# A 2-layer gated and dilated-attention block and a second attention block on one core: the opening loads x ahead of constants and side inputs, sums squares in pairs, and takes the lambda products later

## The chip, the cores and the metric

The kernel runs on one core of one Trainium2 chip. The metric is the device time of one execution in microseconds. Three timed runs of the kernel before gave 1493.45, 1486.89 and 1493.67 us, median 1493.45. The execution that was profiled took 1486.86 us.

## The reference, cut to what matters

The reference applies two blocks to 512 tokens of width 1024. The first is a gated MLP layer and a dilated-attention layer, the second holds a forgetting attention, a differential attention and a feed-forward part. Each layer starts by a root-mean-square norm of x and a modulation by vectors that a conditioning input `c` gives. Only the start of the first layer and one scalar of the second block are touched here:

```python
def gmlp_layer(x, c, ada_w, ada_b, norm_g, w_in, sgu_g, w_s, b_s, w_out):
    shift, scale, gate = ada_mod(c, ada_w, ada_b, 3)      # silu(c) @ w + b, split
    h = rms_norm(x, norm_g) * (1 + scale) + shift         # x * rsqrt(mean(x*x) + EPS) * g ...
    u, v, z = jnp.split(h @ w_in, 3, axis=-1)             # 1024 -> 3 * 2048
    v = rms_norm(jax.nn.gelu(v), sgu_g)
    ...
# second block, used only in its differential attention:
lv = diff_lam[l].astype(jnp.float32)
lam = jnp.exp(jnp.sum(lv[0] * lv[1])) - jnp.exp(jnp.sum(lv[2] * lv[3])) + lam_init
```

## The kernel before, in words

x is kept transposed in SBUF as 8 tiles of 128 model columns by 512 tokens (`x[:, kt, :]`, kt from 0 to 7), and stays there to the end. Weights come in 1 MB chunks (`w_raw`), which ScalarE rounds to `w_hi` and VectorE subtracts to `w_lo` (`to_hi` L486, `to_lo` L910), so that each product is three TensorE matmuls. The modulation vectors come from products of `ada` weight tiles with silu(c) on VectorE, summed along the row (`unit` L918, `up_unit` L1037). The order is written out by hand: each engine has its own instruction list, and waits on semaphores at constants. DMAs are issued in order by SP (queue q1) and by ScalarE (queue q10).

The opening is this. SP issues (L390 to L398) c, the vectors `vecs` (gains and modulation biases), x in two halves of 1 MB, the first `ada_up` tile of 1 MB, two `w_first` chunks of 1 MB, then seven more `ada_up`. ScalarE issues (L527 to L532) the constants (identity, the all-ones tile, masks and EPS, 590 KB), `lam_rows` (128 KB), `bf_col`, `wf_raw` (32 KB) and `csil[1]`, which is c of the second block spread over 128 rows (512 KB).

TensorE spreads c over 128 rows by two matmuls with a one-row operand (L1603), and ScalarE takes silu of both halves (L536). ScalarE then loads its exp and log table (L537) and squares the 8 tiles of x as their half lands (L540). VectorE takes six small gains of `vecs` (L1051 to L1056), waits for the three small inputs (L1057), makes the two lambda products (L1059), and adds squares 1 to 6 one by one onto square 0 (L1065). TensorE sums over the rows by two matmuls with the all-ones tile: one over the sum, one over square 7 (L1606, L1608); its result is signalled by `sum_done`. ScalarE takes Ln, Exp and Square of it (`rstd_start` L493), VectorE ends the reciprocal root by one Newton step (`rstd_end` L953). Then, for each kt, VectorE multiplies x by it (`x_n`, L1070) and makes the two modulation sums of the tile (`up_unit`), ScalarE makes `h_full` (L550) and rounds it to `h_hi` (L552). TensorE takes each `h_full` tile into eight 256-column matmuls against `w_first` in full fp32 (L1629), two records each in the profile. This is the first part of the v projection. VectorE makes the `h_lo` tiles behind the loop (L1076).

After that loop ScalarE issues `ws_t` and `b_sp` (L554, L555, 512 KB each) and goes on to the gelu of the first v tiles (L565). VectorE masks `ws_t` by the causal constant (L1087), which needs both loads. The second value derived from the lambda products, `neg_lam`, was made at L1078 and is read only in the second block.

The lines that the diff touches and their names: `consts` and `K_*` (L105), SP's list (L390), ScalarE's list (L527 to L556 and behind L597), VectorE's list (L1050 to L1078, L1087, L1101, L1128), TensorE's list (L1604).

## Time and profile before

| | us |
|---|---|
| three timed runs | 1486.89, 1493.45, 1493.67 |
| the profiled execution | 1486.86 |
| its span on the core | 1485.1 |
| TensorE busy | 1447.9 (97%) |
| VectorE busy | 953.3 (64%) |
| ScalarE busy | 624.3 (42%) |
| mean granted TensorE clock | 0.996 |

The span is what the profile shows on the engines; the rest of the profiled execution's time, 1.76 us, lies around it. Engines are PE (TensorE matmul), PEld (its weight load), DVE (VectorE), ACT (ScalarE), POOL (GpSimd) and SP. A name such as ACTq stands for the issue of a DMA on that engine. L1519 is the helper that issues every matmul and L908 the helper of VectorE's three-operand operations, so these are told apart by their tiles.

### The profile page before, as it was taken

The page shows a single profiled execution, that of the slowest core. Times are in us where ns is not written, and L with a number is a line of the kernel's source. Part 1 is how long each engine was busy: PE and PEld are TensorE (multiplying, and loading weights), DVE is VectorE, ACT ScalarE, POOL GpSimd, SP SyncE. Part 2 cuts the span into 40 slices and gives each one's busy share as a digit, 9 for nine tenths or more (in the row PEclk, how much of TensorE's full clock was granted, in tenths as well). Part 3 has the DMA queues.
Part 4 walks back from the last instruction along what each step waited for, and adds up shares of the span by engine and source line. Part 5 has one row for each costly group of instructions (what it writes and reads, how often), then busy time and mean ns, then how long its engine had stood idle before and what let it go on. Part 6 is the DMA issues. An engine that isn't in the chain of part 4 may idle for free.

```text
span 1485.1 us, 19595 instructions
## 1 busy us (share of the span) xinstructions
PE 1447.9 (97%) x7404; PEld 1183.0 (80%) x7404; DVE 953.3 (64%) x1392; ACT 624.3 (42%) x916; POOL 124.8 (8%) x58
## 2 busy tenths in 40 slices
PE   5999999999999999999999999999899999999999
PEld 3998888888788688888877787777488888888887
DVE  5975777777888466666666868779777344332333
ACT  4734223332466444444444456655555232211221
POOL 0000100001100322222212100000020000000000
PEclk9999999999999999999999999999999999999999
DMA  9785544467622111111111232012021322222222
GB/s 378 302 344 201 185 183 170 169 242 284 265 75 86 61 63 51 56 55 56 57 57 57 85 115 86 29 60 84 1 102 70 113 85 103 95 98 101 85 92 78
DMA packets 34269, 181.06 MB, mean 122 GB/s; under 512 B 3865, under 2 KB 4121, under 8 KB 19618
## 3 DMA queue, kind: packets, MB, share of 16 engines
q1 hardware_dynamic: 32114, 175.22, 32.0%
q10 hardware_dynamic: 2096, 5.04, 1.0%
q8 instruction: 38, 0.62, 0.2%
q14 instruction: 21, 0.17, 0.0%
HBM read 178.14 MB, written 2.11 MB: 121 GB/s over the span
## 4 chain that ended last, share of the span: by engine, by line
PE 87%; DVE 6%; DMA 4%; issue 1%; ACT 1%; SPq 0%; ACTq 0%; DVEq 0%
PE acc L1519 75%; PE ada L1519 4%; PE norm L1519 4%; DMA ada_out<-in_ada 3%; PE turn L1519 2%; PE turn L1754 1%; DVE w_lo L915 1%; PE turn L1873 1%; DVE hx L908 1%; DMA wf_raw<-in_forget 1%; DVE hk_lo L908 0%; DVE s L908 0%; DVE ada_out L908 0%; DVE h_lo L908 0%; DVE stat L1373 0%
## 5 line engine op out<-in xcount | busy, mean ns | idle before, releaser
L1519 PE MATMUL acc<-h_hi,w_hi 128*128 128x512 f32 x984 | 400.8, 407 | 0.0
L1519 PE MATMUL acc<-h_hi,w_lo 128*128 128x512 f32 x984 | 383.8, 390 | 0.0
L1519 PE MATMUL acc<-h_lo,w_hi 128*128 128x512 f32 x984 | 383.5, 390 | 0.0
L915 DVE TENSOR_TENSOR w_lo<-w_raw,w_hi 128x2048 fp32r<-128x2048 f32 (+1 forms) x89 | 205.9, 2314 | 69.0 <-ACT w_hi L491 68.8
L491 ACT ACTIVATE w_hi<-w_raw 128x2048 fp32r<-128x2048 f32 (+1 forms) x106 | 200.7, 1893 | 117.1 <-PE acc L1519 117.0
L1519 PEld LDWEIGHTS acc<-h_hi,w_hi 128*128 128x128 f32 x984 | 184.9, 188 | 46.1 <-issue 9.0
L1519 PEld LDWEIGHTS acc<-h_lo,w_hi 128*128 128x128 f32 x984 | 185.0, 188 | 44.6 <-issue 8.1
L1519 PEld LDWEIGHTS acc<-h_hi,w_lo 128*128 128x128 f32 x984 | 184.7, 188 | 39.1
L445 POOL TENSOR_TENSOR w_lo<-w_raw,w_hi 128x2048 fp32r<-128x2048 f32 x17 | 77.3, 4548 | 322.4 <-ACT w_hi L491 322.4
L1519 PE MATMUL acc<-w_hi,h_hi 128*128 128x256 f32 x320 | 92.6, 289 | 0.0
L1519 PE MATMUL acc<-w_lo,h_hi 128*128 128x256 f32 x320 | 90.5, 283 | 0.0
L1519 PE MATMUL acc<-w_hi,h_lo 128*128 128x256 f32 x320 | 90.4, 283 | 0.0
L908 DVE SCALAR_TENSOR_TENSOR x<-acc,mods,x 128x512 f32<-128x512 f32 (+1 forms) x40 | 33.1, 829 | 82.4 <-PE acc L1519 82.4
L1519 PE MATMUL acc<-gu_hi,w_hi 128*128 128x512 f32 x176 | 68.5, 389 | 0.0
L1519 PE MATMUL acc<-gu_lo,w_hi 128*128 128x512 f32 x176 | 68.5, 389 | 0.0
L1519 PE MATMUL acc<-gu_hi,w_lo 128*128 128x512 f32 x176 | 68.5, 389 | 0.0
L908 DVE SCALAR_TENSOR_TENSOR gu<-tanh_g,acc 128x512 f32<-128x512 f32 x21 | 14.4, 688 | 82.9 <-PE acc L1519 82.8
L908 DVE SCALAR_TENSOR_TENSOR y_half<-norm,y_half 128x512 f32<-128x512 f32 x54 | 37.1, 687 | 47.1 <-ACT y_half L501 47.1
L1519 PEld LDWEIGHTS acc<-w_hi,h_hi 128*128 128x128 f32 x320 | 61.3, 191 | 3.3 <-issue 3.3
L884 ACT ACTIVATE gu_hi<-gu 128x512 f32 (+1 forms) x22 | 13.9, 633 | 117.1 <-DVE gu L908 117.1
L1519 PEld LDWEIGHTS acc<-w_lo,h_hi 128*128 128x128 f32 x320 | 61.3, 192 | 0.5 <-issue 0.5
L497 ACT ACTIVATE y<-norm,consts 128x512 f32<-128x512 f32 x54 | 37.0, 685 | 58.1 <-PE norm L1519 58.0
(256 smaller groups left out, 2574.7 us busy)
## 6 DMA issues: line engine op xcount, KB each, us to landing
w_raw<-in_weights SPq DMA_DIRECT2D x102, 1024.0 KB, 4.7
ada_v<-in_ada SPq DMA_DIRECT2D x32, 512.0 KB, 5.9
ada_raw<-in_ada SPq DMA_DIRECT2D x32, 512.0 KB, 6.0
ada_out<-in_ada SPq DMA_DIRECT2D x32, 512.0 KB, 6.4
ada_up<-in_ada_first SPq DMA_DIRECT2D x8, 1024.0 KB, 20.2
w_raw<-in_weights SPq DMA_DIRECT2D x4, 768.0 KB, 4.2
x<-in_x SPq DMA_DIRECT2D x2, 1024.0 KB, 9.4
w_first<-in_weights SPq DMA_DIRECT2D x2, 1024.0 KB, 16.3
```

The source lines that it names most:

```text
L445: nc.gpsimd.tensor_tensor(w_lo[par][:, :], w_raw[par][:, :], w_hi[par][:, :].bitcast(F32), ALU.subtract).then_inc(lo_done, 1)
L491: nc.scalar.activation(w_hi[par][:, 0:used], w_raw[par][:, 0:used], ACT.Copy).then_inc(hi_done, 1)
L497: nc.scalar.activation(y0[:, :], total, ACT.Ln, scale=1.0 / count, bias=eps_col).then_inc(ln_done, 1)
L884: nc.scalar.activation(gu_hi[:, f, :], gu[par][:, :], ACT.Copy).then_inc(guhi_done, 1)
L908: return nc.vector.scalar_tensor_tensor(out, in0, scalar, in1, op0, op1, **more)
L915: nc.vector.tensor_tensor(w_lo[par][:, 0:used], w_raw[par][:, 0:used], f32(w_hi[par][:, 0:used]), ALU.subtract)\
L1519: return nc.tensor.matmul(out, lhsT, rhs, start=start, stop=stop)
L1754: turned = nc.tensor.transpose(bank, s_b[:, P * b:P * b + P], ident)
L1873: turned = nc.tensor.transpose(T0[:, P * b:P * b + P], s_2[n % 3][:, 0, P * b:P * b + P], ident)
```

## The change

The constants are laid out anew, with the all-ones tile and EPS in front. ScalarE's opening loads only these 132 columns (128 partitions x 528 bytes), with a semaphore of their own. The rest of the constants, `csil[1]`, `lam_rows`, `bf_col` and `wf_raw` are issued behind the h loop, around `ws_t`. SP issues both halves of x ahead of `vecs`. The squares are added in four pairs, each into its even tile, and TensorE sums the four pair tiles by four matmuls. The exp and log table is loaded behind the squares. The lambda products stand behind the masking of `ws_t`, their Exp and `neg_lam` behind the statistics of v.

```diff
--- before.py
+++ after.py
@@ -98,14 +98,15 @@
     d = i + TOK - P - x
     slopes = np.broadcast_to(-np.array(SLOPES_B, np.float32), (P, 24))
     last = np.broadcast_to(np.array([EPS, 0.0, 0.0, 0.0]), (P, 4))
-    tiles = [ident, ones, half, causal_t, np.where(d >= 0, d, FAR), np.where(i >= j, 0.0, -FAR), slopes, last]
+    tiles = [ones, last, ident, half, causal_t, np.where(d >= 0, d, FAR), np.where(i >= j, 0.0, -FAR), slopes]
     return [np.concatenate(part, axis=1).astype(np.float32) for part in (tiles, blocks)]
 
 
-K_ID, K_ONE, K_HALF, K_TRI, K_DIST, K_MASK = 0, P, 2 * P, 3 * P, 4 * P, 4 * P + TOK
+K_ONE, K_EPS, K_ID = 0, P, P + 4
+K_HALF, K_TRI, K_DIST = K_ID + P, K_ID + 2 * P, K_ID + 3 * P
+K_MASK = K_DIST + TOK
 K_SLOPE = K_MASK + P
-K_EPS = K_SLOPE + 24
-NCONST = K_EPS + 4
+NCONST = K_SLOPE + 24
 
 
 def program(nc, d):
@@ -250,7 +251,7 @@
     def sem(name):
         return nc.alloc_semaphore(name)
 
-    vecs_loaded, consts_loaded, ws_loaded = sem("vecs_loaded"), sem("consts_loaded"), sem("ws_loaded")
+    vecs_loaded, ones_loaded, consts_loaded, ws_loaded = sem("vecs_loaded"), sem("ones_loaded"), sem("consts_loaded"), sem("ws_loaded")
     x_loaded = [sem("x_loaded0"), sem("x_loaded1")]
     small_loaded, blocks_loaded, stored = sem("small_loaded"), sem("blocks_loaded"), sem("stored")
     w_loaded = [sem("w_loaded0"), sem("w_loaded1")]
@@ -388,9 +389,9 @@
                 sp.dma_start(ada_up[kt % UP][:, :, :].rearrange("p e k -> p (e k)"), d["ada_first"][kt]).then_inc(ada_up_loaded[kt % UP], 16)
 
             sp.dma_start(c_in[:, :], d["c"]).then_inc(c_loaded, 16)
-            sp.dma_start(vecs[:, :], d["vecs"]).then_inc(vecs_loaded, 16)
             for half in range(2):
                 sp.dma_start(x[:, 4 * half:4 * half + 4, :], d["x"][:, 4 * half:4 * half + 4, :]).then_inc(x_loaded[half], 16)
+            sp.dma_start(vecs[:, :], d["vecs"]).then_inc(vecs_loaded, 16)
             ada_up_load(0)
             for par in range(2):
                 sp.dma_start(w_first[par][:, :, :].rearrange("p k n -> p (k n)"), weights[par]).then_inc(w_first_loaded[par], 16)
@@ -524,23 +525,16 @@
                 nc.scalar.activation(sq[m % 2][:, :], x[:, m, :], ACT.Square).then_inc(sq_ready, 1)
 
 
-            act.dma_start(consts[:, :], d["tiles"]).then_inc(consts_loaded, 16)
-            act.dma_start(lam_rows[:, :], d["diff_lam_2"][0].rearrange("a b -> (a b)").partition_broadcast(P)).then_inc(small_loaded, 16)
-            act.dma_start(bf_col[:, :], d["b_f_2"].rearrange("a h -> h a")).then_inc(small_loaded, 16)
-            act.dma_start(wf_raw[:, :, :], d["forget"]).then_inc(small_loaded, 16)
-
-            act.dma_start(csil[1][:, :], d["c_2"][0].partition_broadcast(P)).then_inc(c2_loaded, 16)
+            act.dma_start(consts[:, 0:K_ID], d["tiles"][:, 0:K_ID]).then_inc(ones_loaded, 16)
 
             for n in range(2):
                 act.wait_ge(c_spread_in, n + 1)
                 nc.scalar.activation(csil[0][:, TOK * n:TOK * n + TOK], G[n][:, :], ACT.Silu).then_inc(csil_ready, 1)
-            act.preload_act_table_set("natural_log_exp_and_others")
             for kt in range(KT):
                 act.wait_ge(x_loaded[kt // 4], 16)
                 nc.scalar.activation(sq_first[kt][:, :], x[:, kt, :], ACT.Square).then_inc(sq_ready, 1)
+            act.preload_act_table_set("natural_log_exp_and_others")
             rstd_start(N_X0, NB[:, :], DM)
-            act.wait_ge(lam_part, 2)
-            nc.scalar.activation(lam_two[:, :], lam_two[:, :], ACT.Exp).then_inc(lam_exp, 1)
             for kt in range(KT):
                 if kt == KT - 1:
                     to_hi(1, 0)
@@ -551,7 +545,12 @@
                 act.wait_ge(hx_done, kt + 1)
                 nc.scalar.activation(h_hi[:, kt, :], h_full[:, kt, :], ACT.Copy).then_inc(hhi_done, 1)
 
+            act.dma_start(csil[1][:, :], d["c_2"][0].partition_broadcast(P)).then_inc(c2_loaded, 16)
+            act.dma_start(consts[:, K_ID:NCONST], d["tiles"][:, K_ID:NCONST]).then_inc(consts_loaded, 16)
             act.dma_start(ws_t[:, :, :], d["spatial"]).then_inc(ws_loaded, 16)
+            act.dma_start(lam_rows[:, :], d["diff_lam_2"][0].rearrange("a b -> (a b)").partition_broadcast(P)).then_inc(small_loaded, 16)
+            act.dma_start(bf_col[:, :], d["b_f_2"].rearrange("a h -> h a")).then_inc(small_loaded, 16)
+            act.dma_start(wf_raw[:, :, :], d["forget"]).then_inc(small_loaded, 16)
             act.dma_start(b_sp[:, :, :], d["a_b_spatial"][0].rearrange("g t -> (g t)").partition_broadcast(P)
                           .rearrange("p (g t) -> p g t", g=GROUPS)).then_inc(small_loaded, 16)
 
@@ -595,6 +594,8 @@
             nc.scalar.activation(v_stat[:, 2, :], v_stat[:, 1, :], ACT.Exp, scale=-0.5).then_inc(v_stat_act, 1)
             act.wait_ge(v_stat_act, 2)
             nc.scalar.activation(v_stat[:, 3, :], v_stat[:, 2, :], ACT.Square, scale=math.sqrt(0.5 / AW)).then_inc(v_stat_act, 1)
+            act.wait_ge(lam_part, 2)
+            nc.scalar.activation(lam_two[:, :], lam_two[:, :], ACT.Exp).then_inc(lam_exp, 1)
 
 
             def uz_pair(u):
@@ -1047,6 +1048,10 @@
                 stt(gscale[:, kt:kt + 1], mods[:, SCALE_A + 2 * kt:SCALE_A + 2 * kt + 1], 1.0, vecs[:, G_A + kt:G_A + kt + 1],
                     ALU.add, ALU.mult).then_inc(gsa_done, 1)
 
+            for i in range(KT // 2):
+                dve.wait_ge(sq_ready, 2 * i + 2)
+                nc.vector.tensor_tensor(sq_first[2 * i][:, :], sq_first[2 * i][:, :], sq_first[2 * i + 1][:, :], ALU.add)\
+                    .then_inc(sq_added, 1 + i // 2)
             dve.wait_ge(vecs_loaded, 16)
             nc.vector.tensor_scalar(gains[:, 0:1], vecs[:, G_QB:G_QB + 1], P ** -0.5, None, ALU.mult)
             nc.vector.tensor_scalar(gains[:, 1:2], vecs[:, G_FQ:G_FQ + 1], 0.125, None, ALU.mult)
@@ -1054,15 +1059,6 @@
             nc.vector.tensor_scalar(gains[:, 3:4], vecs[:, G_DQ:G_DQ + 1], 0.125, None, ALU.mult)
             nc.vector.tensor_copy(gains[:, 4:5], vecs[:, G_DK:G_DK + 1])
             nc.vector.tensor_scalar(gains[:, 5:6], vecs[:, G_DN:G_DN + 1], 1.0 - LAM_INIT, None, ALU.mult).then_inc(gains_ready, 1)
-            dve.wait_ge(small_loaded, 48)
-            for n in range(2):
-                stt(lam_prod[:, 64 * n:64 * n + 64], lam_rows[:, 128 * n:128 * n + 64], 1.0,
-                    lam_rows[:, 128 * n + 64:128 * n + 128], ALU.mult, ALU.mult, accum_out=lam_two[:, n:n + 1]).then_inc(lam_part, 1)
-            for m in range(1, KT - 1):
-                dve.wait_ge(sq_ready, m + 1)
-                if m > 1:
-                    dve.wait_ge(sq_added, m - 1)
-                nc.vector.tensor_tensor(sq_first[0][:, :], sq_first[0][:, :], sq_first[m][:, :], ALU.add).then_inc(sq_added, 1)
             dve.wait_ge(csil_ready, 2)
             up_unit(0)
             rstd_end(N_X0, NB[:, :], DM, x_rstd)
@@ -1074,8 +1070,6 @@
             for kt in range(KT):
                 dve.wait_ge(hhi_done, kt + 1)
                 nc.vector.tensor_tensor(h_lo[:, kt, :], h_full[:, kt, :], f32(h_hi[:, kt, :]), ALU.subtract).then_inc(hlo_done, 1)
-            dve.wait_ge(lam_exp, 1)
-            stt(neg_lam[:, :], lam_two[:, 1:2], -LAM_INIT, lam_two[:, 0:1], ALU.add, ALU.subtract).then_inc(lam_ready, 1)
 
 
             ada_v_units(0, 0)
@@ -1085,6 +1079,10 @@
             dve.wait_ge(consts_loaded, 16)
             tri = consts[:, K_TRI:K_TRI + P].unsqueeze(1).broadcast_to([P, GROUPS, P])
             nc.vector.tensor_tensor(ws_t[:, :, :], ws_t[:, :, :], tri, ALU.mult).then_inc(ws_ready, 1)
+            dve.wait_ge(small_loaded, 64)
+            for n in range(2):
+                stt(lam_prod[:, 64 * n:64 * n + 64], lam_rows[:, 128 * n:128 * n + 64], 1.0,
+                    lam_rows[:, 128 * n + 64:128 * n + 128], ALU.mult, ALU.mult, accum_out=lam_two[:, n:n + 1]).then_inc(lam_part, 1)
             ada_v_units(1, 0)
             to_lo(2, 0)
             ada_v_units(1, 1)
@@ -1099,6 +1097,8 @@
             stt(v_stat[:, 4, :], v_stat[:, 0, :], AW * EPS, v_stat[:, 3, :], ALU.add, ALU.mult).then_inc(v_stat_dve, 1)
             dve.wait_ge(v_stat_dve, 2)
             stt(v_stat[:, 5, :], v_stat[:, 4, :], 1.5, v_stat[:, 2, :], ALU.subtract, ALU.mult, reverse0=True).then_inc(v_stat_dve, 1)
+            dve.wait_ge(lam_exp, 1)
+            stt(neg_lam[:, :], lam_two[:, 1:2], -LAM_INIT, lam_two[:, 0:1], ALU.add, ALU.subtract).then_inc(lam_ready, 1)
 
 
             def uz_pair(u, cond):
@@ -1125,7 +1125,6 @@
                                             f32(y_hi[:, j, :]).rearrange("p (c t) -> p c t", c=TB),
                                             ALU.subtract).then_inc(ylo_done, 1)
 
-            dve.wait_ge(small_loaded, 64)
             half_uz = W_UZ // 2 + (C2_UNIT - FIRST_UZ_UNIT) // (2 * UNITS_UZ)
             uz_pair(W_UZ // 2, 0)
             with dve.Fori(W_UZ // 2 + 1, half_uz) as u:
@@ -1601,11 +1600,11 @@
             pe.wait_ge(c_loaded, 16)
             for n in range(2):
                 mm(G[n][:, :], one_row[:, :], c_in[:, TOK * n:TOK * n + TOK], True, True).then_inc(c_spread_in, 1)
-            pe.wait_ge(consts_loaded, 16)
-            pe.wait_ge(sq_added, KT - 2)
-            mm(NB[:, :], ones, sq_first[0][:, :], True, False)
-            pe.wait_ge(sq_ready, KT)
-            mm(NB[:, :], ones, sq_first[KT - 1][:, :], False, True).then_inc(sum_done, 1)
+            pe.wait_ge(ones_loaded, 16)
+            for i in range(KT // 2):
+                pe.wait_ge(sq_added, (1, 2, 4, 6)[i])
+                last = mm(NB[:, :], ones, sq_first[2 * i][:, :], i == 0, i == KT // 2 - 1)
+            last.then_inc(sum_done, 1)
 
 
             def v_pair(u):
```

## Rows read from the trace of the kernel before

**Rows 1.** The page: busy time by engine; granted clock by slice; the last chain's shares.

```profile
PE 1447.9 (97%) x7404; PEld 1183.0 (80%) x7404; DVE 953.3 (64%) x1392; ACT 624.3 (42%) x916; POOL 124.8 (8%) x58
...
PEclk9999999999999999999999999999999999999999
...
PE 87%; DVE 6%; DMA 4%; issue 1%; ACT 1%; SPq 0%; ACTq 0%; DVEq 0%
```

**Rows 2.** The chain in order of time, opening (start us, us, what).

```profile
2.29 9.19 DMA wf_raw<-in_forget
...
11.50 0.38 DVE lam_prod L908 x4
11.88 0.62 DVE sq_first L1065
...
15.78 0.70 DVE sq_first L1065
16.48 0.14 issue
16.62 3.58 PE norm L1519 x4
20.19 5.17 issue
25.36 1.19 PE acc L1519 x2
26.55 0.85 PE turn L1519 x2
...
31.40 0.43 PE acc L1519 x2
...
55.58 14.51 PE acc L1519 x121
```

**Rows 3.** Timeline of the opening (start us, us, instructions, idle before and releaser).

```profile
1.14 0.37 SPq L391 DMA_DIRECT2D vecs<-in_vecs  x1
...
1.57 0.89 SPq L393 DMA_DIRECT2D x<-in_x  x2
...
2.41 3.75 PE L1519 MATMUL acc<-c_in,one_row 1*128 1x512 f32 x4 [2.41 <-DMA c_in<-in_c]
...
5.18 0.14 DVE L1056 TENSOR_SCALAR gains<-vecs 128x1 f32<-128x1 f32 x1
6.19 0.60 ACT L536 ACTIVATE csil<-acc 128x512 f32<-128x512 f32 x1 [1.07 <-PE acc L1519]
6.80 1.28 ACT L537 ACT_TABLE_LOAD   x1
9.51 2.19 ACT L540 ACTIVATE sq_first<-x 128x512 f32<-128x512 f32 x4 [1.42 <-DMA x<-in_x]
...
12.97 2.19 ACT L540 ACTIVATE sq_first<-x 128x512 f32<-128x512 f32 x4 [1.27 <-DMA x<-in_x]
16.39 1.22 DVE L908 SCALAR_TENSOR_TENSOR ada_up<-ada_up,csil 128x1024 f32<-128x1024 f32 x1
...
18.99 0.16 DVE L908 SCALAR_TENSOR_TENSOR gscale<-mods,vecs 128x1 f32<-128x1 f32 x1
...
34.17 0.68 DVE L1070 TENSOR_TENSOR x_n<-x,x_rstd 128x512 f32<-128x512 f32 x1
...
37.45 0.68 DVE L1070 TENSOR_TENSOR x_n<-x,x_rstd 128x512 f32<-128x512 f32 x1
```

**Rows 4.** Stretches: us, busy PE, PEld, DVE, ACT, POOL, PEclk, DMA share, GB/s.

```profile
3.00:3.50 0.50, 0.50 (x2) 0.11 (x1) 0.00 (x0) 0.27 (x1) 0.00 (x0) 1.00 1.01 406
...
4.50:5.00 0.50, 0.50 (x1) 0.08 (x1) 0.14 (x3) 0.49 (x2) 0.00 (x0) 1.00 0.49 57
...
10.00:15.00 5.00, 0.00 (x0) 0.00 (x0) 3.08 (x9) 3.73 (x8) 0.00 (x0) 1.00 1.02 425
...
25.00:30.00 5.00, 4.64 (x11) 3.77 (x12) 4.93 (x11) 2.33 (x4) 0.00 (x0) 0.50 1.02 423
```

**Rows 5.** The DMAs: the page's issues; tile x; issues from 27 to 50 us.

```profile
w_raw<-in_weights SPq DMA_DIRECT2D x102, 1024.0 KB, 4.7
...
DMA to landing us min/median/max: 7.9/9.4/10.9
...
ada_up<-in_ada_first SPq DMA_DIRECT2D x1, 1024.0 KB, 11.5
```

**Rows 6.** DMA packets by queue from 3 to 3.5 us, then from 5 to 5.5 us.

```profile
q10 hardware_dynamic: 43, 0.20, 100.5%
...
q10 hardware_dynamic: 31, 0.03, 46.3%
q1 hardware_dynamic: 4, 0.03, 16.4%
```

**Rows 7.** Timeline behind the opening.

```profile
4.09 23.57 SPq L388 DMA_DIRECT2D ada_up<-in_ada_first  x7
...
48.68 0.45 ACTq L555 DMA_DIRECT2D b_sp<-in_a_b_spatial  x1
...
53.02 0.38 ACT L565 ACTIVATE v<-acc 128x256 f32<-128x256 f32 x1 [2.58 <-PE turn L1519]
...
55.77 0.28 PE L1519 MATMUL acc<-w_hi,h_hi 128*128 128x256 f32 x1
...
58.04 0.28 PE L1519 MATMUL acc<-w_lo,h_hi 128*128 128x256 f32 x1
...
70.06 1.23 DVE L908 SCALAR_TENSOR_TENSOR ada_v<-ada_v,csil 128x1024 f32<-128x1024 f32 x1 [1.14 <-DMA ada_v<-in_ada]
...
74.97 2.29 DVE L915 TENSOR_TENSOR w_lo<-w_raw,w_hi 128x2048 fp32r<-128x2048 f32 x1
```

**Rows 8.** Stretch of 54 to 56 us (columns as in rows 4).

```profile
54.00:56.00 2.00, 2.00 (x13) 1.82 (x12) 2.00 (x5) 1.97 (x10) 0.00 (x0) 1.00 0.00 0
```

## The prediction

> **What bounds the kernel now.** I read the page first. TensorE is busy 97% of the span, its granted clock is near full in every slice, and it holds 87% of the chain that ended last [rows 1]. So only what shortens TensorE's own work, or lets it start sooner, moves the end. All edits but two small ones lie ahead of 77 us, so I read the chain in order of time next [rows 2]. It starts at the landing of `wf_raw` at 11.48 us, a small load of the second block that VectorE waits for ahead of its adds. The lambda products and six adds follow up to 16.48, two matmuls over the squares take 3.58, then 5.17 us pass to the first h matmul at 25.36. From there TensorE issues without a gap past 55.58. The reader is to see that nothing from c, the constants or the modulation weights stands on this chain, only a load that the opening's arithmetic doesn't use. Whatever brings the first h matmul forward moves all that follows, so long as loads and VectorE keep up with it.
>
> **When x lands.** x's two halves are issued from 1.57 us and land 7.9 and 10.9 us after their issue [rows 3, 5]: 9.5 and 12.9 us, which fits the squares' starts at 9.51 and 12.97 [rows 3]. Queue q10 (ScalarE's) holds all DMA engines from 3 to 3.5 us, and x's queue q1 has four packets from 5 to 5.5 us [rows 6]; around 4.5 us the engines are half busy and move 57 GB/s [rows 4]. With only the 66 KB of ones ahead and `vecs` behind, x goes out one place earlier, at 1.14 [rows 3]. A 1 MB load in the steady part lands in 4.7 us [rows 5], and one more MB takes 2.5 us at 425 GB/s [rows 4]: I take 5.8 us for the first half and 8.3 for the second. The other end is that x's slowness is its own: 1.14 + 7.9 = 9.0 and 12.5 us.
>
> The Trainium skill bears on this. In "DMA: Bandwidth & Descriptors", section "Queues, rings and completion order", it says that each DMA engine goes round-robin between queues that have work. By that rule x was slowed only by the bytes that shared the engines with it, and its own descriptors weren't late. Rows 6 speak against an even sharing in this opening: from 3 to 3.5 us only q10 has packets, though x was issued at 1.57. By the rule x would gain only the bytes that leave its way, some 1.2 MB or 2.8 us at 425 GB/s, and land near 7.2 and 9.8 us, and the total gain below would be some 4.0 us in place of 4.9.
>
> **The squares and their sum.** ScalarE ends the second silu at 6.79 and now squares at once, since the table load (1.28 us) goes behind the squares [rows 3]. There it runs beside the pair sums on TensorE; without that cover it would cost its 1.28. Four squares take 2.19 us [rows 3], so eight run from 6.8 to about 11.1. An add is 0.70 [rows 2]. Pair 0 is ready at 6.8 + 1.1 + 0.7 = 8.6, pair 1 at 9.7, pair 2 at 10.8, pair 3 at 11.9. VectorE has four adds in place of six and waits for no small load.
>
> TensorE now makes four matmuls and not two. Two took 3.58 us, so 1.79 each; the same kind of work at 256 columns takes 0.85 at the slow rate and 0.43 at the other [rows 2], with the granted clock at 0.50, which is 1.2 GHz, from 25 to 30 us [rows 4] and full in nearly all of the page's slices [rows 1]. A 512-column one at 1.79 is thus at the 1.2 GHz level. Four of them from 8.65 end at 8.65 + 7.16 = 15.8, and TensorE is their bound, not VectorE. If the clock rises while they run, as it did after 4.6 us of unbroken h matmuls in rows 2 and 4, the last ends by 14.4 to 14.9. If all ran at 2.4 GHz the end would be pair 3 plus one matmul, 11.9 + 0.9 = 12.8. Against 20.20 in the trace the sum comes 4.4 (all slow), 5.8 (last one and a half fast) or 7.4 us (all fast) earlier. I take 4.9, near the slow end, because both short bursts on TensorE in the opening (3.75 and 3.58 us) ran slow throughout [rows 3, 2].
>
> **From the sum to the first h matmul** the chain is unchanged: Ln, Exp, Square, two Newton steps, x_n, h_full, 5.17 us [rows 2]. The first `up_unit` and the gains must be done by then. The gains wait for `vecs`, now behind x, near 8.6 us, and come behind the adds at 11.9, and take 0.4 us; `up_unit(0)` took 16.39 to 19.15 [rows 3], 2.8 us, so 12.3 to 15.1, while VectorE's next work is due at 15.3 + 2.1. Covered; without the cover up to 0.4. The first h matmul moves from 25.36 to about 20.5.
>
> **The h loop.** TensorE needs 8 x 0.43 = 3.45 us for a tile at full clock and VectorE makes one each 3.28 us (34.17 to 37.45) [rows 2, 3]. TensorE stays the bound, hence the shift is kept. In the first 4.6 us the clock is low [rows 4], which costs 2.3 us now and will again; a shorter or longer low stretch moves the result by up to 1 us either way. Supply: DMA runs full at about 425 GB/s [rows 4], and `ada_up` 7, issued at 27.3, landed 11.5 us later at 38.8 [rows 7, 5]. SP's order makes `ada_up` 1 the sixth MB behind x's first half: counting back six times 2.47 us from 38.8, it landed at 24.0, just ahead of its use at 24.9. In the change x's second half is in at 8.3, then `vecs` (0.2) and four MB: 18.4 us, for a use at 24.93 - 4.9 = 20.0. The loads gain as much as the work, since 1.2 MB left their way. If x lands late, so do these, and so does the work.
>
> **The moved loads.** Seven DMAs are issued behind the h loop in place of two. Five issues of the kind took 0.36 to 0.60 us each, 2.3 us together, against ScalarE's wait of 2.58 us ahead of the first gelu [rows 7]. That just fits; without cover they'd delay the gelu, which TensorE needs only at its next accumulators, so I count zero, at most 0.5. Their extra 1.2 MB (524 KB of the constants, then 128, 32 and 512 KB) take 2.9 us of DMA time, where the engines now stand still from 54 to 56 us [rows 8], with the new loads done by about 51. Zero.
>
> **Lambda.** The products (0.38 us [rows 2]) go behind the mask of `ws_t`, where VectorE waits 1.14 us for `ada_v` [rows 7]: hidden. Their Exp and `neg_lam` stand behind the statistics of v, one tiny operation each like the gains (0.14 us [rows 3]), on engines that TensorE is not waiting for: zero, at most 0.3.
>
> **Sum.** -4.9 us, bounds -2.1 (x not earlier) to -7.4. From the profiled execution, 1486.86 us (1485.1 in the span), that is 1482.0. The three runs shown lie at two values: one agrees with the profiled one, two are 6.6 us above, for no reason that a trace shows. The median is one of the upper ones, so I forecast 1493.45 - 4.9 = 1488.5, and count the lower value, 1482.0, as nearly as likely.
>
> **Rivals.**
> 1. *x lands no earlier* (the change doesn't do what it says). For: before 5 us q1 moves next to nothing [rows 6]. Against: 57 GB/s around 4.5 us, with small packets of q10, says that q10 was in the way [rows 4]. Squares from 9.0, the first pair at 10.9, four slow matmuls end at 18.0: -2.1 us, 1491.3. By an even sharing of the engines -4.0, 1489.5. Together 0.20.
> 2. *TensorE is warm during the pair sums*, so that the squares set the end: -7.4 us, 1486.0 (1479.5 at the lower value). For: the four matmuls are one unbroken stretch of up to 7 us after the c matmuls. Against: both bursts of the opening ran slow. 0.12.
> 3. *Slower: the masking of `ws_t` waits.* VectorE now waits there for the constants and four small loads, issued last. Behind it stand the `ada_v` units and `w_lo` of the fifth chunk, which ends at 77.26; TensorE gets to it at 55.58 + 2 x 96 x 0.12 = 78.6 [rows 2, 7], where 0.12 is the spacing of 20 matmuls from 55.77 to 58.04. Each us by which these loads are late beyond 1.1 (the wait that is there) plus 1.3 costs one. To turn the gain into a loss they must land 7.3 us after VectorE gets there at 62.8, which is 26 us after their issue near 44; x in the crowded opening took 10.9 [rows 5]. 1495 us at 8 us late, 0.05.
> 4. The forecast, -3.5 to -6.4 us: 0.63.
>
> **Chances.** Against 1493.45 a change under 0.5% (7.5 us) can't be told from none. The gain by itself is 0.33%, so it falls within 0.5% unless the new kernel's median lies at the lower value, as it did in one of three runs and in the profiled one; I give that 0.42, most of all cases. Slower by over 0.5% only by rival 3: 0.05. The rest, 0.53, is no change. The range: 1480.5 (the forecast at the lower value, part of rival 2) to 1492.5 (rival 1 and a delayed gelu). The forecast's own range at the upper value is 1487 to 1490.
>
> **What would show it.** Right: squares in one run from about 6.8 us, `x` landing 4.7 and 7.2 us after issue, four norm matmuls without a gap from about 8.7 to 15.3, first h matmul near 20.5, the w_hi matmuls starting near 50.7 in place of 55.58, no wait ahead of L1087's successor. Wrong: a second square group that starts after 10 us, norm matmuls at 0.9 us each, a wait of VectorE for `ada_up`, or a gap of TensorE between 60 and 90 us.

## The result: some 6.4 us faster in the median, and the profile after

| | runs | median us | lowest to highest |
|---|---|---|---|
| before | 17 | 1489.58 | 1486.27 to 1493.67 |
| changed | 17 | 1483.14 | 1480.09 to 1487.30 |

The ratio is 0.9955, 95% interval 0.9944 to 0.9966: 5.1 to 8.3 us faster. Each kernel's own runs spread over 7 us, as much as the gain; the last part of the experiments says why. The profiled execution of the changed kernel took 1483.83 us, with a span of 1482.0, 3.1 under the span before.

The chain of the changed kernel in order of time (start us, us, what) answers to [rows 2]:

```profile
0.75 1.40 DMA c_in<-in_c
2.28 3.76 PE acc L1518 x4
6.06 0.60 ACT csil L532
6.66 1.04 ACT sq_first L535 x2
7.73 0.70 DVE sq_first L1053
8.57 5.95 PE norm L1518 x8
14.52 5.17 issue
19.68 1.19 PE acc L1518 x2
20.88 0.85 PE turn L1518 x2
...
23.44 0.48 PE acc L1518 x2
23.91 0.43 PE ada L1518 x2
```

No load of the second block heads it now. It starts with c, which TensorE spreads and ScalarE puts through silu, then two squares and one add; from 8.57 us TensorE has norm matmuls without a gap. The step of 5.17 us is untouched.

The timeline of the changed kernel (columns as in rows 3):

```profile
1.15 0.84 SPq L393 DMA_DIRECT2D x<-in_x  x2
...
6.06 0.60 ACT L532 ACTIVATE csil<-acc 128x512 f32<-128x512 f32 x1 [1.11 <-PE acc L1518]
6.56 4.25 ACT L535 ACTIVATE sq_first<-x 128x512 f32<-128x512 f32 x8
...
10.83 1.28 ACT L536 ACT_TABLE_LOAD   x1
10.91 0.69 DVE L1053 TENSOR_TENSOR sq_first<-sq_first,sq_first 128x512 f32<-128x512 f32 x1 [0.34 <-ACT sq_first L535]
...
11.89 1.22 DVE L909 SCALAR_TENSOR_TENSOR ada_up<-ada_up,csil 128x1024 f32<-128x1024 f32 x1
...
46.24 1.28 ACT L564 ACT_TABLE_LOAD   x1 [2.97 <-issue]
47.53 0.38 ACT L564 ACTIVATE v<-acc 128x256 f32<-128x256 f32 x1
...
49.27 0.38 PE L1518 MATMUL acc<-w_hi,h_hi 128*128 128x256 f32 x1
...
63.36 0.22 DVE L909 SCALAR_TENSOR_TENSOR lam_prod<-lam_rows 128x64 f32<-128x64 f32 x1
```

The eight squares run as one group, with no wait for x in between, where the old ones had two waits [rows 3]. The table load stands behind them, beside TensorE. The first gelu starts the moment its table load ends, with no wait for TensorE ahead of it, where it had waited 2.58 us before [rows 7]. The lambda products have no wait ahead of them.

How long x took in the changed kernel (to compare with rows 5):

```profile
DMA to landing us min/median/max: 4.9/6.0/7.0
```

The two halves of x, issued at 1.15 and near 1.6 us, landed near 6.05 and 8.6 us. A stretch of the same trace (columns as in rows 4) shows the DMA engines full already at 3.5 us:

```profile
3.50:4.00 0.50, 0.50 (x1) 0.10 (x1) 0.00 (x0) 0.00 (x0) 0.00 (x0) 1.00 1.01 426
```

### The profile page after: what moved, and what is told of

It is laid out like the page before. It is cut to its first block, busy times and chain, and to the rows that moved or that the text cites. A ratio compares the mean times of both kernels' runs of the same rounds, so it can differ in the third digit from the quotient of the medians.

```text
span 1482.0 us, 19599 instructions
## 1 busy us (share of the span) xinstructions
PE 1452.7 (98%) x7408; PEld 1185.6 (80%) x7408; DVE 952.0 (64%) x1390; ACT 624.1 (42%) x916; POOL 124.9 (8%) x58
## 3 DMA queue, kind: packets, MB, share of 16 engines
q10 hardware_dynamic: 2240, 5.04, 1.1%
## 4 chain that ended last, share of the span: by engine, by line
PE 89%; DVE 5%; DMA 3%; issue 1%; ACT 1%; SPq 0%; DVEq 0%; ACTq 0%
PE acc L1518 76%; PE ada L1518 4%; PE norm L1518 4%; DMA ada_out<-in_ada 3%; PE turn L1518 2%; PE turn L1753 1%; DVE w_lo L916 1%; PE turn L1872 1%; DVE s L909 1%; DVE ada_out L909 0%; DVE stat L1372 0%; DVE hx L909 0%; DVE h_lo L909 0%; DVE s_b L909 0%; DVE z_t L1226 0%
## 5 line engine op out<-in xcount | busy, mean ns | idle before, releaser
L885 ACT ACTIVATE gu_hi<-gu 128x512 f32 (+1 forms) x22 | 13.9, 633 | 117.1 <-DVE gu L909 117.1
L1518 PEld LDWEIGHTS acc<-w_hi,h_lo 128*128 128x128 f32 x320 | 61.3, 192 | 0.0
```

What stands on the lines that cost most here:

```text
L885: nc.scalar.activation(gu_hi[:, f, :], gu[par][:, :], ACT.Copy).then_inc(guhi_done, 1)
L1518: return nc.tensor.matmul(out, lhsT, rhs, start=start, stop=stop)
```

## The experiments

In all of them "first h" is the first matmul over `h_full` (25.36 us before, 19.68 in the changed kernel) and "the seam" the first w_hi matmul, right behind the h loop (55.23 and 49.27).

### Taking the parts away

**The lambda products alone** (kernel before, with the products, their Exp and `neg_lam` moved as in the change):

```diff
-            dve.wait_ge(small_loaded, 48)
...
             for m in range(1, KT - 1):
```

> The kernel before with one edit: the lambda products, their Exp and neg_lam stand where the change puts them; the order of the loads, the six serial adds and the two matmuls over the squares are the old ones. Theory A (the wait for wf_raw only covers other waits: squares 4 to 7 come at 13.5 to 15.1 us because x's second half lands at 12.9): the serial adds then end at about 15.9 in place of 16.48, the sum of squares at 19.6 in place of 20.20, first h matmul 24.8 in place of 25.36, about -0.6 us. Rival B (the load that heads the chain of waits is the cost; the chain gives its landing 9.2 us): the adds go with the first squares, at least 2 us come back, first h matmul below 23.4.

```profile
12.43 2.19 ACT L540 ACTIVATE sq_first<-x 128x512 f32<-128x512 f32 x4 [0.82 <-DMA x<-in_x]
13.09 2.29 DVE L1061 TENSOR_TENSOR sq_first<-sq_first,sq_first 128x512 f32<-128x512 f32 x3 [0.20 <-ACT sq_first L540]
15.53 3.75 PE L1518 MATMUL norm<-sq_first,consts 128*128 128x512 f32 x4 [9.26 <-DVE sq_first L1061]
```

These are rows of its timeline. First h came at 24.45, 0.9 us earlier and not 2; median 1490.23, ratio 1.0000 (0.9987 to 1.0014). The adds wait for the squares, and the squares for x's second half. Of the 0.9 us, 0.5 is that x's second half came sooner in this execution (squares at 12.43, and 12.97 before), which the edit doesn't explain; that leaves 0.4 for the move, near theory A's 0.6. The load that headed the old chain with 9.2 us was one of several that ended together.

**The old order of loads** (changed kernel; `vecs` ahead of x, all of ScalarE's loads at the start):

```diff
+            sp.dma_start(vecs[:, :], d["vecs"]).then_inc(vecs_loaded, 16)
             for half in range(2):
                 sp.dma_start(x[:, 4 * half:4 * half + 4, :], ...)
-            sp.dma_start(vecs[:, :], d["vecs"]).then_inc(vecs_loaded, 16)
...
+            act.dma_start(consts[:, K_ID:NCONST], d["tiles"][:, K_ID:NCONST]).then_inc(consts_loaded, 16)
...
```

> The changed kernel with the loads issued in the old order (vecs ahead of x; all constants, the small inputs and c of the second block at the start of ScalarE's queue). Pairs, four matmuls, late table load and late lambda stay. Theory A (x's landing is the larger part): x lands near 9.5 and 12.9 us, the first pair at 11.3, the norm matmuls start at 11.4 and end between 17.3 and 18.5, first h matmul 22.5 to 23.7: -1.7 to -2.9 us of the change's -5.7. Rival B (the wait for the small loads and the serial adds were the cost, not x): first h matmul below 21.

```profile
8.49 2.19 ACT L540 ACTIVATE sq_first<-x 128x512 f32<-128x512 f32 x4 [1.64 <-DMA x<-in_x]
11.84 2.19 ACT L540 ACTIVATE sq_first<-x 128x512 f32<-128x512 f32 x4 [1.16 <-DMA x<-in_x]
```

First h came at 22.40, 2.7 us behind the changed kernel, a hair before the range. Median 1487.14, ratio 0.9978 (0.9967 to 0.9990). The norm matmuls started at 10.51 and took 6.71. x didn't go back to its old times: its halves landed near 8.5 and 11.8, a us before those of the kernel before (9.5 and 12.9), with the same loads around them (only the constants come in two pieces). At the seam the loads are worth more, 3.9 us (53.12 against 49.27), for VectorE waited 1.04 us for the second `ada_up`, and TensorE 0.64 for `h_lo`.

**The old serial sum** (changed kernel with the six adds and two matmuls):

```diff
-                nc.vector.tensor_tensor(sq_first[2 * i][:, :], sq_first[2 * i][:, :], sq_first[2 * i + 1][:, :], ALU.add)
+                nc.vector.tensor_tensor(sq_first[0][:, :], sq_first[0][:, :], sq_first[m][:, :], ALU.add)
...
```

> The changed kernel with the old serial sum: six adds onto square 0 and two matmuls. Loads in the new order. Theory A: squares run from 6.6 to 10.8 us as in the changed kernel, the adds, 0.79 us apart, from 7.7 to 12.4, two matmuls at the slow rate 3.6 us, sum at 16.1, first h matmul 21.3 in place of 19.68: the pairs are worth 1.6 us, the rest of the change 4.1. Rival B (TensorE's rate rises only because four matmuls keep it busy, and more of the gain hangs on it): the h loop too starts slower or ends over 2 us later than in the changed kernel.

```profile
7.93 4.67 DVE L1055 TENSOR_TENSOR sq_first<-sq_first,sq_first 128x512 f32<-128x512 f32 x6 [7.93 <-ACT sq_first L535]
...
12.75 3.75 PE L1519 MATMUL norm<-sq_first,consts 128*128 128x512 f32 x4 [6.52 <-DVE sq_first L1055]
```

First h came at 21.67 (21.3 expected): the pairs are worth 2.0 us. Median 1486.58, ratio 0.9981 (0.9966 to 0.9996). The adds ran at their own pace, six in 4.67 us, as theory A said.

**The table load ahead of the squares** (changed kernel):

```diff
+            act.preload_act_table_set("natural_log_exp_and_others")
             for kt in range(KT):
                 act.wait_ge(x_loaded[kt // 4], 16)
                 nc.scalar.activation(sq_first[kt][:, :], x[:, kt, :], ACT.Square).then_inc(sq_ready, 1)
-            act.preload_act_table_set("natural_log_exp_and_others")
```

> The changed kernel with the exp and log table loaded ahead of the squares, as before. Theory A (ScalarE is the bound of the opening's first 9 us now, as x lands at 6.05 before it ends silu at 6.66): squares start at 7.9 in place of 6.56, the first pair 1.3 us later, norm matmuls 1.3 us later, first h matmul 20.6 to 21.0 in place of 19.68. Rival B (x's landing or TensorE sets the sum, the table load is hidden in either place): under 0.4 us of difference.

First h came at 21.37, 1.7 us late and beyond the 21.0 forecast. 0.25 of it is that the second silu came later in this execution (6.31 and not 6.06), so the placement of one 1.28 us load is worth about its length. It was free before only because x was late: ScalarE waited 1.42 us behind it [rows 3]. Median 1484.59, ratio 0.9968 (0.9952 to 0.9984), within the noise of the changed kernel.

Counted one at a time from the full change, the loads give 2.7 us, the pairs 2.0 and the table 1.7. The lambda move gives 0.9 by itself, counted from the other end, so the four don't form a sum; each was hidden behind another. Each is a difference of two single profiles, and two profiles of the changed kernel itself put first h at 19.68 and 20.25 (last part), so each can be off by some 0.6 us.

### What bounds the changed opening

**Two sums of four** (VectorE adds the pairs once more, TensorE makes two matmuls):

```diff
+                if i % 2 == 1:
+                    quad(i // 2, 3 * (i // 2) + 2)
```

> The changed kernel with the four pair sums added once more on VectorE to two sums of four, and two norm matmuls in place of four. Theory A (TensorE at its slow rate is the bound of the sum of squares: first pair at 8.4, then 5.95 us of matmuls without a gap): VectorE ends the second sum of four near 12.4, two matmuls at 1.8 us run 10.3 to 12.1 and 12.4 to 14.2, sum at 14.2 in place of 14.52, first h matmul 19.2 to 19.6. Rival B (VectorE's chain sets the sum): first h matmul over 20.2.

Norm matmuls from 10.49 to 14.31, first h 19.48, seam 49.31. Halving the matmuls moved first h by 0.2 us and the seam by nothing, which is within what two profiles of one kernel differ by; median 1484.49, ratio 0.9965 (0.9951 to 0.9980). Two slow matmuls later are as good as four earlier ones, as theory A said.

**TensorE kept busy ahead of the norm matmuls:**

```diff
+            for _ in range(6):
+                mm(T0[:, 0:P], ones, ones, True, True)
```

> The changed kernel with six 128-column fp32 matmuls of ones by ones, whose result nobody reads, between the c matmuls and the norm matmuls, so that TensorE is busy from 6.0 us on. Theory A (the norm matmuls are slow because TensorE stood idle before them): the granted clock rises 1.5 to 3 us earlier, the norm matmuls end near 13.3 in place of 14.52, first h matmul near 18.5; the h loop still begins at 1.2 GHz after the idle 5.17 us and loses its 2 us. Rival B (the rise takes matmuls of other data or comes at a time of its own): norm matmuls still 5.9 us, the fill delays them by up to 0.3.

The norm matmuls took 5.24 us in place of 5.95 and first h came at 19.07, half of what theory A promised. Median 1484.69, ratio 0.9965 (0.9948 to 0.9981). One profile of each isn't enough to price this fill. Over all kernels with the four pairs and the new loads, the norm matmuls took 5.95, 6.37 and 5.22 us without it (the third is the next kernel, whose fill stands behind them) and 5.24, 4.44, 4.13, 4.16 and 5.04 with it: about 1.2 us less in the mean.

**TensorE kept busy between the sum and the first h matmul:**

```diff
+            def fill(cols):
+                mm(T0[:, 0:cols], ones, x[:, 0, 0:cols], True, True)
+            fill(512)
+            for gate in (ln_done, y0_done, half_done, newton_done):
+                pe.wait_ge(gate, 1)
+                fill(256)
...
```

> The changed kernel with matmuls whose result nobody reads in the 5.17 us between the sum of squares and the first h matmul: one of 512 columns, then one of 256 behind each step of the reciprocal root (Ln, Exp, Square, both Newton steps), about 0.43 us of work in each 0.7. Theory A (the h loop starts at 1.2 GHz because TensorE idles 5.17 us): the clock stays at 2.4 GHz from 13.4 on, the first h tile takes 3.45 us in place of 5.4, and the end of the h loop comes 1.9 us earlier: -1.9 us in all against the changed kernel. Rival B (VectorE's 3.28 us a tile or the ada_up loads take over): under 1 us. Rival C (a half-busy TensorE does not hold its clock): nothing, or up to 0.5 us slower.

The timeline of this kernel, and its waits (engine, tile, line, waited for: us in total, times, longest):

```profile
18.93 0.67 PE L1518 MATMUL acc<-w_first,h_full 128*128 128x256 f32 x2 [0.92 <-issue]
19.11 1.23 DVE L909 SCALAR_TENSOR_TENSOR ada_up<-ada_up,csil 128x1024 f32<-128x1024 f32 x1 [0.52 <-DMA ada_up<-in_ada_first]
19.44 0.59 PE L1518 MATMUL turn<-w_first,h_full 128*128 128x256 f32 x2
...
43.90 4.90 DVE L1072 TENSOR_TENSOR h_lo<-h_full,h_hi 128x512 fp32r<-128x512 f32 x8
...
49.14 0.38 PE L1518 MATMUL acc<-w_hi,h_hi 128*128 128x256 f32 x1 [1.86 <-DVE h_lo L1072]
```

```profile
PEld acc L1518 <- ACT v L564: 2.3, 1, 2.3
...
PE acc L1518 <- DVE h_lo L1072: 1.9, 1, 1.9
```

The h loop ran at 2.4 GHz from its first matmuls (0.43 us apart, and not 0.85). It took 1.4 us less (28.3 and not 29.7), and its end came 2.1 us earlier; the other 0.7 us was there at first h already, from the shorter norm matmuls, which this fill can't have made. All of it was given back at the seam: 49.14 against 49.27. There TensorE waits for VectorE's last `h_lo`, done at 48.80. The wait view puts the weight load's 2.3 us down to the first gelu, but the two tiles that this load needs were out at 48.32; with the gelu 5 us ahead (three kernels on) the view still names it. What the matmul follows is `h_lo`: it starts 0.34 us behind its end here, with both fills and in both GpSimd kernels.

Why was `h_lo` no earlier? In the changed kernel its eight tiles ran from 44.04 to 48.94, here from 43.90 to 48.80. They follow VectorE's eight `x_n` and `up_unit` steps of 3.28 us each, and a faster TensorE doesn't shorten those; and of the 0.76 us by which the first `x_n` came earlier (17.29, and 18.05 in the changed kernel), 0.52 went to a wait for the second `ada_up`. These are the two things that rival B named, VectorE's pace and the load; they only show at the seam, as `h_lo`. So theory A holds for the clock, and rival B for the sum. Median 1481.96, ratio 0.9956 (0.9940 to 0.9973).

**Both fills:**

```diff
+            for _ in range(6):
+                mm(T0[:, 0:P], ones, ones, True, True)
...
+            for gate in (ln_done, y0_done, half_done, newton_done):
+                pe.wait_ge(gate, 1)
+                fill(512)
...
```

> Both fills, and 512 columns in place of 256 at each step of the gap. Theory A: the norm matmuls end near 13.3 and the h loop starts near 18.5 at 2.4 GHz: -1.2 and -1.9, together -3.1 us against the changed kernel, about 1480.0 us in the median, -9.5 against the kernel before. Rival B (the ada_up loads are the next bound: in the changed kernel they land with the same lead as before): VectorE waits for ada_up in the h loop and the gain is under 2 us.

```profile
18.31 0.67 PE L1518 MATMUL acc<-w_first,h_full 128*128 128x256 f32 x2 [0.26 <-issue]
...
19.02 1.22 DVE L909 SCALAR_TENSOR_TENSOR ada_up<-ada_up,csil 128x1024 f32<-128x1024 f32 x1 [1.05 <-DMA ada_up<-in_ada_first]
...
49.06 0.38 PE L1518 MATMUL acc<-w_hi,h_hi 128*128 128x256 f32 x1 [1.87 <-DVE h_lo L1072]
```

First h 18.31, and now VectorE waits 1.05 us for `ada_up`, which came near 19.0 as in the gap fill; the seam is where it was. Median 1481.13, ratio 0.9948 (0.9929 to 0.9968), not told apart from the changed kernel's.

**Part of h_lo on GpSimd** (the kernel with both fills):

```diff
+            pool.wait_ge(gsa_done, KT)
+            for kt in range(3):
+                pool.wait_ge(hhi_done, kt + 1)
+                nc.gpsimd.tensor_tensor(h_lo[:, kt, :], h_full[:, kt, :], h_hi[:, kt, :].bitcast(F32), ALU.subtract)
...
```

> The kernel with both fills, and the first three h_lo tiles made by GpSimd behind VectorE's last gscale. In the run with both fills TensorE ended its h loop some 2.2 us ahead of the changed kernel and gave nearly all of it back at the seam to the first w_hi matmul: h_lo is done at 48.7 there, and ScalarE's first gelu, behind seven DMA issues and a table load, at 48.2. Theory A (VectorE's h_lo is last at the seam, the gelu next, 0.5 us behind): the w_hi matmuls start 0.4 to 0.7 us earlier than with both fills and then wait for the gelu. Rival B (h_lo alone holds the seam): 1.5 to 2 us earlier. Rival C (GpSimd and VectorE slow each other): not earlier.

```profile
41.36 6.22 POOL L466 TENSOR_TENSOR h_lo<-h_full,h_hi 128x512 fp32r<-128x512 f32 x3 [40.42 <-DVE gscale L913]
...
41.41 3.37 DVE L920 TENSOR_TENSOR w_lo<-w_raw,w_hi 128x2048 fp32r<-128x2048 f32 x1
44.70 5.23 DVE L1076 TENSOR_TENSOR h_lo<-h_full,h_hi 128x512 fp32r<-128x512 f32 x5
...
50.27 0.38 PE L1522 MATMUL acc<-w_hi,h_hi 128*128 128x256 f32 x1 [3.28 <-DVE h_lo L1076]
```

Rival C. While GpSimd makes three tiles in 6.22 us, VectorE's `w_lo` takes 3.37 in place of 2.29 and its five `h_lo` tiles 5.23 where eight took 4.90. The seam came at 50.27, 1.2 us later than with both fills, and in the trace the clock fell once more behind the idle 3.3 us. Median 1488.47, ratio 0.9987 (0.9972 to 1.0001): most of the change's gain lost.

**The same, with four DMA issues behind the first gelu tiles and `ada_up` 1 ahead of the second `w_first`:**

```diff
+            v_chunk(0, 0, True)
+            act.dma_start(lam_rows[:, :], ...).then_inc(small_loaded, 16)
...
+            v_chunk(0, 1, True)
...
+                if par == 0:
+                    ada_up_load(1)
```

> As the run before, and four of the seven DMA issues (lam_rows, bf_col, wf_raw, b_sp, 2.1 us together) go behind the first gelu tiles, and the second ada_up tile is loaded ahead of the second w_first chunk. Theory A (the moved issues hold the gelu, and ada_up 1 holds VectorE for 1.05 us with both fills): gelu no later than 46.5, VectorE's wait for ada_up gone, the w_hi matmuls start near 47, that is -1.8 us against both fills and -8 us against the kernel before at that place; median near 1479.5. Rival B (another wait at the seam, such as w_first 1 landing later or h_hi): under 1 us.

The gelu started at 44.15, and at 47.69 in the run before, so the moved issues were most of what held it. VectorE's wait for `ada_up` is down from 1.17 to 0.39 us. But `h_lo` still held the seam, at 49.57: with the gelu tiles out 4.8 us ahead of it, TensorE waited 3.5 us. Median 1486.66, ratio 0.9976 (0.9963 to 0.9989).

**A wait for each h_lo tile, no work on GpSimd** (the kernel with both fills; the four late DMA issues and the early `ada_up` 1 of the last kernel stay, so three things differ from both fills):

```diff
-            h_ready(0, KT - 1)
...
+                        for kt in range(KT):
+                            if (par, hb, t) == (0, 0, 0):
+                                h_ready(0, kt)
+                            last = rows(..., (kt,))
```

> The kernel with both fills, with VectorE making all h_lo again. TensorE's first w_hi chunk is written out and waits for each h_lo tile as it comes to it, not for the eighth ahead of all; four DMA issues go behind the first gelu tiles; the second ada_up tile is loaded ahead of the second w_first chunk. Theory A (the seam holds TensorE only by the wait for all h_lo and by the late gelu; the fills' 2.2 us lie behind them): the w_hi matmuls start near 46.9 with no wait over 0.5 us, 8 us or more ahead of the kernel before at that place, and stay so to 320 us; median 1480 to 1481.5, 2 us under the changed kernel. Rival B (a further wait takes the place: ScalarE's gelu, or the next w_lo chunks): at 60 us no more than 6.6 us ahead. Behind 400 us each further stretch at 1.2 GHz takes some 1.5 us back.

```profile
46.38 0.59 PE L1520 MATMUL norm<-w_first,h_full 128*128 128x256 f32 x2
46.63 0.47 PE L1520 MATMUL acc<-w_hi,h_hi 128*128 128x256 f32 x1
46.93 0.28 PE L1520 MATMUL acc<-w_lo,h_hi 128*128 128x256 f32 x1
```

TensorE passes the seam without a wait, at 46.63: 8.6 us ahead of the kernel before, 2.6 ahead of the changed one. VectorE still ended its `h_lo` at 48.37, so the wait that was gone is the one for all eight tiles. Followed by ScalarE's activations, 0.6 of the lead is lost by 90 us, and 8.0 us are still there at 300 us (292.77 against 300.72). Median 1482.61 of six runs, ratio 0.9943 (0.9922 to 0.9965), against 0.9957 (0.9942 to 0.9972) for the changed kernel on the same chip. It is the best ratio of all, and the runs don't tell it from the changed kernel; the 1480 to 1481.5 that theory A forecast was missed.

### Where the runs' spread comes from

**The changed kernel again**, unedited:

> The changed kernel again, unedited, on the chip of the run before it. If the differences behind 400 us are stretches at 1.2 GHz that fall differently in each execution, then its opening is again 6.0 us ahead at 60 us within 0.1, its end is that less 1.4 to 1.6 us for each such stretch beyond the kernel before's one, and its median lies 5 to 7 us under that of the kernel before. If they are an effect of the change, its end is again 3.1 us ahead with three stretches at the same places.

Stretches of the changed kernel's first profile, then of this one (columns as in rows 4):

```profile
400.00:420.00 20.00, 20.00 (x125) 18.14 (x124) 18.13 (x23) 13.13 (x13) 0.00 (x0) 0.91 0.15 53
1045.00:1085.00 40.00, 33.99 (x185) 21.51 (x182) 30.41 (x71) 19.44 (x46) 0.00 (x0) 0.91 0.08 27
1120.00:1140.00 20.00, 20.00 (x106) 17.09 (x105) 18.23 (x26) 10.27 (x13) 0.00 (x0) 1.00 0.18 63
```

```profile
400.00:420.00 20.00, 20.00 (x125) 18.05 (x124) 18.14 (x23) 13.07 (x13) 0.00 (x0) 0.91 0.14 53
1045.00:1085.00 40.00, 33.83 (x187) 22.31 (x182) 30.49 (x71) 19.36 (x46) 0.00 (x0) 0.91 0.08 27
1120.00:1140.00 20.00, 20.00 (x92) 17.02 (x91) 18.00 (x26) 10.37 (x13) 0.00 (x0) 0.83 0.17 57
```

One kernel, two executions, spans of 1482.0 and 1485.2 us. In the second the granted clock is at 1.2 GHz also between 1120 and 1140 us, for 6.8 of the 20 us (0.83). The opening wasn't the same either, against my 0.1 us: the norm matmuls took 6.37 and not 5.95, first h 20.25, seam 49.84.

Over all profiles, the lead on the kernel before at the seam, the lead at the end (1485.1 less the span), their difference, and the granted clock in the three stretches:

| kernel | lead at seam | lead at end | given back | clock 400, 1045, 1120 |
|---|---|---|---|---|
| before | 0 | 0 | 0 | 1.00, 0.96, 1.00 |
| table first | 4.3 | 4.9 | -0.6 | 0.91, 1.00, 1.00 |
| both fills | 6.2 | 5.8 | 0.4 | 0.83, 1.00, 1.00 |
| front fill | 6.4 | 5.3 | 1.1 | 0.91, 1.00, 0.91 |
| old loads | 2.1 | -0.2 | 2.3 | 0.91, 0.91, 1.00 |
| serial adds | 4.0 | 1.7 | 2.3 | 0.91, 0.91, 1.00 |
| lambda alone | 1.2 | -1.5 | 2.7 | 0.91, 0.91, 1.00 |
| changed | 6.0 | 3.1 | 2.9 | 0.91, 0.91, 1.00 |
| changed again | 5.4 | -0.1 | 5.5 | 0.91, 0.91, 0.83 |
| quads | 5.9 | 0.1 | 5.8 | 0.91, 0.91, 0.83 |
| gap fill | 6.1 | -1.0 | 7.1 | 0.83, 0.91, 0.83 |
| GpSimd | 5.0 | 0.9 | 4.1 | 1.00, 0.91, 0.91 |
| GpSimd, late issues | 5.7 | 0.8 | 4.9 | 0.83, 0.91, 1.00 |
| each h_lo tile | 8.6 | 2.4 | 6.2 | 0.91, 0.87, 0.91 |

What is given back behind the seam goes with the time at 1.2 GHz. That time is twice the stretch times what the clock lacks of 1: some 11 us in the changed kernel and 18 in its second profile, against 3 before, so about 0.4 us are lost for each further us in the kernels that gave most back. The two GpSimd kernels lose 1.4 us of theirs within 20 us of the seam. For the others the steps of the lead fall where the clock does: in the second profile of the changed kernel it is 5.3 us at 400 us, 4.2 from 430 to 1040, 3.1 at 1115 and -0.1 from 1150 to the end, by ScalarE's instructions. Near 330 us a little is lost without a low clock, 0.6 us in the changed kernel's first profile.

The timed runs say the same, for each has its mean granted clock on record. Of the eleven runs of this kernel, the five at 0.992 took 1486.15 to 1488.03 us and the four at 0.995 or above 1480.80 to 1482.82. Of the kernel before on the same chip, the six at 0.992 took 1492.34 to 1493.61 and the four at 0.996 1487.16 to 1487.76. So the 7 us of spread go with the clock, and at equal clock the change is worth 6.0 us (medians at 0.992) to 6.6 (at 0.996), near the lead that it has at the seam. What makes an execution fall at one place and not at another stays open.

One caution on the view itself: in the opening the profile's granted clock can't be used to tell the level. It reads 1.00 from 10 to 15 us in all the profiles read there, and 1.00 from 20 to 24 us in that of the serial adds, where TensorE's first h matmuls are 0.85 us apart as they are in the profiles that read 0.50 there. In the opening the level is read from the matmuls' own spacing.

## Why the prediction was right, and where it wasn't

**x's landing**: 5.8 and 8.3 us forecast, 6.05 and 8.6 measured. The round-robin rule of the Trainium skill ("DMA: Bandwidth & Descriptors", "Queues, rings and completion order"), read as a delay by the shared bytes alone, would have had 7.2 and 9.8 by my working. That working is off: 2.8 us off the old landings, 9.5 and 12.9, is 6.7 and 10.1. The changed trace alone is 0.6 and 1.5 us ahead of that, 0.4 of which is the earlier issue. But with the old loads put back x landed near 8.5 and 11.8, so taking them away gave 2.4 and 3.2 us, around the 2.8 of the shared bytes; and there x's queue had 27 packets from 5 to 5.5 us and ScalarE's four, the other way round than in [rows 6]. The landing came out as forecast, but the runs don't decide against the rule, and the two queues shared the engines differently in the two profiles of the crowded opening.

**Squares and pairs**: 6.8 to 11.1 and a last pair at 11.9 forecast; 6.56 to 10.8 and 11.6 measured.

**The four norm matmuls**: 8.65 to 15.3 forecast, 8.57 to 14.52 and 8.72 to 15.09 in the two profiles. TensorE at 1.2 GHz, by the spacing of its matmuls, is their bound for the greater part, and quads and front fill bear it out. Rival 2 (TensorE warm) stays out: all at 2.4 GHz would have ended at 12.8, and only with the front fill did it come near that (12.8 to 13.9).

**From the sum on**: 5.17 us as before. The first `up_unit` was hidden. The forecast of 4.9 us at first h is 5.7 in one profile and 5.1 in the other.

**The h loop** kept the shift and added 0.5 us to it in the first profile, 0.2 of which went at the seam, and 0.3 in the second, inside the 1 us allowed.

**VectorE and the supply behind TensorE** were the weak step. I compared 3.45 us a tile on TensorE with 3.28 on VectorE, called TensorE the bound, and stopped at the end of the loop. But the seam also needs `w_lo` and eight `h_lo` from VectorE, 7.1 us behind its last tile. In the changed kernel `h_lo` was done at 48.94 and the first w_hi matmul started 0.33 us behind it, at 49.27, the same step as in the kernels that wait for it. So the path that the sum left out already sets the seam there, by 0.2 us: 0.48 us lie between the last matmuls of the h loop and the seam, and 0.25 in the kernel before. It holds the seam in every kernel whose TensorE came sooner, but for the one that waits tile by tile. The supply was closer too: I had `ada_up` 1 at 18.4 us, 1.6 ahead of its use (it is the fifth MB behind x's first half, not the sixth). The fills, whose VectorE waits for it, show it at 18.8 to 19.1, and the changed kernel uses it at 19.26.

**The moved loads** had a tighter cover than I gave them. The five added issues took 2.4 us, as forecast, but with the gaps between them 2.7 (3.59 us from the first issue to the table load, 0.85 before), against a wait of 2.58, and I called that a fit. TensorE also ended its h loop 0.5 us earlier still, relative to ScalarE, and the gelu's wait was gone: it started with the end of its table load. It cost nothing, for TensorE needs the gelu only at the seam. Even in the gap fill `h_lo` held TensorE longer than the gelu did, so no run here shows these issues to cost anything.

**Lambda**: no wait at 63.36 us, so rival 3 fell. Rival 1 (x no earlier) fell with x at 6.05.

**The level, not the gain, was wrong.** The measured 1483.14 is 5.4 us under the forecast of 1488.5, and outside its own range of 1487 to 1490. It is inside the range I gave, 1480.5 to 1492.5, only because that covered both values I had seen; that much is luck. My 0.53 for a change under 0.5% came true too, at 0.45%, but I had worked it out from the upper value, which 1483.14 is 0.69% under. I read three runs and a profile as two values 6.6 us apart "for no reason that a trace shows", and forecast 1488.5 from the upper one. Seventeen runs fill the interval from 1486.3 to 1493.7, the median is 1489.58, and the traces do show the reason. The gain of 4.9 us was 6.4 in the medians and is just under the interval of 5.1 to 8.3; the opening alone accounts for 5.4 to 6.0. I took the clock to rise late or not at all in the norm matmuls, and it rose a little earlier, and the h loop gave 0.3 us that I hadn't counted.

## What to carry to other kernels

The load that heads the chain of waits need not be what it costs: taking it off gave 0.9 us of 5.7, because the squares, x and an add chain ended within a us of it; price each by moving it alone. An engine that became early exposes things that were free, here a table load (1.7 us) and VectorE's work at the end of the loop: a fill that made TensorE 1.4 us faster gave nothing, until the wait for all eight tiles was split into one for each. When you compare two engines' pace in a loop, follow both to the next place where they meet. And before a 0.4% gain is read off a profile, look at the granted clock of the whole span: one kernel's two profiles ended 3.2 us apart, 2.6 of them by the clock behind the seam. Comparing runs at equal mean clock takes most of that out.

## What the runs showed of the hardware that I had not expected

- Matmuls with nothing to compute for, between the sum and first h, kept TensorE's next matmuls at 0.43 us and not 0.85, which made the h loop 1.4 us shorter.
- Six 128-column matmuls ahead of the norm matmuls, with no gap behind the c matmuls, left them at 4.13 to 5.24 us; without them one and the same kernel took 5.95 and 6.37.
- GpSimd beside VectorE on plain subtractions slowed VectorE: its 128x2048 took 3.37 and not 2.29 us. GpSimd made three 128x512 tiles in 6.22 us; no run shows what they take alone.
- x moved at full rate from 3.5 us when it was alone (426 GB/s). In the crowded opening its queue had four packets between 5 and 5.5 us in one execution [rows 6] and 27 in the one with the old loads put back.
